# A decoder layer on one core: the gate projection as seven products of block sums instead of eight, its bias laid into the banks first

## What is computed

```python
    h = h + rms_norm(jnp.einsum('bsf,fd->bsd', ff, w_down[i]), mlp_post_g[i])
    gate = jax.nn.sigmoid(jnp.einsum('bsd,de->bse', h, w_ple_gate[i]) + b_ple_gate[i])
    ple = jnp.einsum('bsp,pd->bsd', p[i], w_ple[i]) * gate
    h = h + rms_norm(ple, ple_post_g[i])
```

## Time and profile before

| | |
|---|---|
| median of three runs | 583.5 us |
| the profiled execution: its span from first to last instruction | 581.5 us |
| what the runs' median has beyond that span | 2.0 us |
| TensorE / its weight loads busy | 573.5 / 500.8 us |
| VectorE / ScalarE / POOL busy | 495.2 / 356.4 / 98.6 us |
| first matmul of the gate, end of the last | 529.5, 575.4 us |
| from there to the end of the span | 6.1 us |

### The profile page before, as it was taken

The page is one execution under the profiler, slowest core; times in us unless marked ns, Lnnn a source line. Parts: engine busy times, 40 slices in busy tenths (PEclk is TensorE's granted clock), DMA queues, the critical chain, the costliest instruction groups (busy, mean ns, idle before and its releaser), DMA issues.

```text
span 581.5 us, 8919 instructions
## 1 busy us (share of the span) xinstructions
PE 573.5 (99%) x3400; PEld 500.8 (86%) x3400; DVE 495.2 (85%) x639; ACT 356.4 (61%) x569; POOL 98.6 (17%) x152
## 2 busy tenths in 40 slices
PE   8999999999999999999999999999999999999995
PEld 7888888888888888989999999999989999988885
DVE  5899986688766998999989999999999899799664
ACT  6896675775646746667656665575655756654422
POOL 0331536000103463001010011010100100011011
PEclk9999999999999999999999999999999999999998
DMA  8982008223003559469485492774753936584011
GB/s 269 345 320 85 0 2 324 76 72 123 25 1 109 202 189 319 87 183 229 96 249 114 119 276 41 215 185 74 264 132 75 285 75 155 207 294 178 0 73 73
DMA packets 26250, 89.26 MB, mean 154 GB/s; under 512 B 3040, under 2 KB 4448, under 8 KB 25696
## 3 DMA queue, kind: packets, MB, share of 16 engines
q1 hardware_dynamic: 20448, 66.59, 32.6%
q0 software_dynamic: 4032, 14.68, 14.3%
q10 hardware_dynamic: 1728, 7.42, 3.4%
HBM read 82.40 MB, written 6.29 MB: 153 GB/s over the span
## 4 chain that ended last, share of the span: by engine, by line
PE 98%; DMA 1%; DVE 0%; ACT 0%; SPq 0%; issue 0%; POOL 0%; DVEq 0%; ACTq 0%
PE psum L2340 31%; PE psum L2344 30%; PE psum L2345 30%; PE psum L2395 2%; PE psum L2578 2%; PE psum L2558 2%; DMA first_raw_a<-weights_dram 1%; PE psum L2409 1%; PE psum L2432 0%; DVE h L1323 0%; ACT w_hi L1393 0%; POOL stat L2192 0%; PE psum L2463 0%; PE psum L2457 0%; PE psum L2437 0%
## 5 line engine op out<-in xcount | busy, mean ns | idle before, releaser
L2340 PE MATMUL psum<-t_hi,a_hi 128*128 128x512 f32 x216 | 84.8, 393 | 0.0
L2344 PE MATMUL psum<-t_lo,a_hi 128*128 128x512 f32 x216 | 84.6, 392 | 0.0
L2345 PE MATMUL psum<-t_hi,a_lo 128*128 128x512 f32 x216 | 84.0, 389 | 0.0
L2340 PE MATMUL psum<-w_hi,actT_hi 128*128 128x512 f32 (+1 forms) x190 | 73.6, 387 | 0.0
L2345 PE MATMUL psum<-w_hi,actT_lo 128*128 128x512 f32 (+1 forms) x190 | 72.4, 381 | 0.0
L2344 PE MATMUL psum<-w_lo,actT_hi 128*128 128x512 f32 (+1 forms) x190 | 72.3, 380 | 0.0
L2345 PE MATMUL psum<-sum_hi,up_lo 128*128 128x256 f32 x224 | 63.4, 283 | 0.0
L2344 PE MATMUL psum<-sum_lo,up_hi 128*128 128x256 f32 x224 | 63.4, 283 | 0.0
L2340 PE MATMUL psum<-sum_hi,up_hi 128*128 128x256 f32 x224 | 63.2, 282 | 0.0
L2345 PE MATMUL psum<-actT_hi,up_lo 128*128 128x256 f32 (+1 forms) x200 | 60.0, 300 | 0.0
L2344 PE MATMUL psum<-actT_lo,up_hi 128*128 128x256 f32 (+1 forms) x200 | 60.0, 300 | 0.0
(11 more groups left out here) (264 smaller groups left out, 1415.8 us busy)
## 6 DMA issues: line engine op xcount, KB each, us to landing
raw<-weights_dram SPq DMA_DIRECT2D x34, 512.0 KB, 4.5
raw_o<-weights_dram SPq DMA_DIRECT2D x23, 512.0 KB, 4.3
raw_x<-weights_dram POOLq DMA_DIRECT2D x21, 512.0 KB, 5.6
raw_second<-weights_dram SPq DMA_DIRECT2D x14, 512.0 KB, 4.2
raw_x<-weights_dram SPq DMA_DIRECT2D x9, 512.0 KB, 5.9
qk_raw<-weights_dram SPq DMA_DIRECT2D x8, 512.0 KB, 6.8
gate_raw<-weights_dram SPq DMA_DIRECT2D x8, 512.0 KB, 5.1
raw_o<-weights_dram POOLq DMA_DIRECT2D x7, 512.0 KB, 7.1
```

What stands on the lines that cost most here:

```text
L2340: begin = nc.tensor.matmul(out, a_hi, b_hi, start=first, stop=False, skip_group_check=read_between)
L2344: nc.tensor.matmul(out, a_hi, b_lo, start=False, stop=False, skip_group_check=read_between)
L2345: return nc.tensor.matmul(out, a_lo, b_hi, start=False, stop=last, skip_group_check=read_between)
```

## The change

**The scheme.** h (turned) is cut in 2 x 2 blocks of 256 tokens x 512 k, A11, A12, A21, A22, and the weights in 2 x 2 blocks of 512 x 512. Seven products of blocks and block sums take the place of eight: GATE_11, 21, T1, T2, T3, T4, 22, the T ones with sums of weights. A product is worked for one pair member j of a token half at a time (128 tokens x 512 columns, 12 matmuls), and these 14 halves alternate by `GATE_PRODUCTS`. The last one, (6, 1), is cut in two parts of 256 columns.

**Sums of h.** ScalarE copies each turned bank to SBUF (`h2_copy_raw`) and splits six of the eight (`h2_split_hi`); VectorE's low parts now come from SBUF (`h2_split_lo`). VectorE makes E, S2, S3 and S4 for both j (`h2_sum`), ScalarE and VectorE split each (`h2_sum_split_hi`, `h2_sum_split_lo`).

**Sums of weights.** They are made by loads that add into what is there: four blocks (T1, T2, T3, T4) of two halves, issued by POOL (`add_gate`), each behind VectorE's split of the block before it (T3 behind a plain load), and standing among the four `down_rstd`. Splits are 128x1024 (`gate_split_hi`, `gate_split_lo`), 14 of them.

**Results.** The bias is copied by ScalarE into four banks ahead of the products (`seed_chain`, `seed_e`; POOL adds the two halves of the bias row once), and `gate_bias` is gone. Instead ScalarE drains six banks to `acc` (`gate_copy`), VectorE adds or subtracts (`gate_c11`, `gate_c22`), and `gate_fold` subtracts from banks in place. The nine sigmoid tiles keep their sizes and now come in another order, and token tiles end in the order 2, 0, 3, 1 (`TOKENS_DONE`). `gate_ple`, `gain_ple`, `square_ple`, the roots and `add_ple` are as before for each tile.

**Loads.** The gain row of the MLP, the bias row and the gain row of the embedding have places of their own and are loaded by SP; both ple loads and the last gain row are asked for once the down tiles are complete.

```diff
-GATE_TILES = ((0, 0, W), (1, 0, W), (0, W, W), (1, W, W), (2, 0, W), (2, W, W), (3, 0, W),
-              (3, W, W // 2), (3, W + W // 2, W // 2))
+GATE_TILES = ((0, 0, W), (1, 0, W), (2, W, W), (2, 0, W), (3, W, W), (0, W, W), (3, 0, W),
+              (1, W, W // 2), (1, W + W // 2, W // 2))
+TOKENS_DONE = (2, 0, 3, 1)
...
+GATE_PRODUCTS = ((0, 0), (1, 0), (0, 1), (1, 1), (2, 0), (3, 0), (2, 1), (4, 0), (3, 1), (5, 0), (4, 1), (6, 0),
+                 (5, 1), (6, 1))
...
             # VectorE
+            def h2_sum(which, j):
+                a11, a12, a21, a22 = h2_block(0, 0, j), h2_block(0, 1, j), h2_block(1, 0, j), h2_block(1, 1, j)
+                if which == OF_E:
+                    dve.wait_ge(h2_raw, 6 + 2 * j)
+                    first, second, how = a21, a22, ALU.subtract
...
+                nc.vector.tensor_tensor(gate_sum_source(which, j), first, second, how).then_inc(x_summed, 1)
+            def gate_c11(j):
+                dve.wait_ge(c_copied, gate_copy_at(COPY_C11, j))
+                dve.wait_ge(up_filled, gate_at(1, j))
+                part = acc[:, j, 0:W]
+                nc.vector.tensor_tensor(part, part, psum[:, GATE_P1 + j, :], ALU.add).then_inc(c_summed, 1)
...
-            for i, (t, c0, width) in enumerate(GATE_TILES):
-                gate_bias(i)
...
+            gate_c11(0)
+            gate_split_lo(GATE_T3, 0)
+            gate_split_lo(GATE_T3, 1)
...
+            h2_sum(OF_S3, 1)
+            gate_split_lo(GATE_T4, 0)
...
+            gate_ple(3)
+            gate_c22(1)
+            add_ple(2)
+            gate_ple(4)
+            gain_ple(4)
+            gate_ple(5)
+            add_ple(0)
+            gate_ple(6)
+            add_ple(3)
+            gate_ple(7)
+            gain_ple(7)
+            gate_ple(8)
+            add_ple(1)
...
             # ScalarE
+            def h2_copy_raw(i):
+                t, k_half = divmod(i, 2)
...
+                nc.scalar.activation(h2_block(t // 2, k_half, t % 2), h2_turned(i), ACT.Copy).then_inc(h2_raw, 1)
...
+            gate_copy(COPY_E, 0)
+            gate_copy(COPY_CHAIN, 0)
+            gate_split_hi(GATE_T4, 0)
...
+            for i in range(4, len(GATE_TILES)):
                 sigmoid(i)
                 square_ple(i)
...
             # POOL
+            add_gate(GATE_T1, 0)
+            add_gate(GATE_T1, 1)
+            pool.wait_ge(bias_loaded, 16)
+            nc.gpsimd.tensor_tensor(gate_bias_row[:, W:2 * W], gate_bias_row[:, 0:W], gate_bias_row[:, W:2 * W],
+                                    ALU.add).then_inc(bias_summed, 1)
+            add_gate(GATE_T2, 0)
+            down_rstd(0)
+            add_gate(GATE_T2, 1)
+            down_rstd(1)
+            down_rstd(2)
+            add_gate(GATE_T3, 0)
+            down_rstd(3)
+            add_gate(GATE_T3, 1)
+            add_gate(GATE_T4, 0)
+            add_gate(GATE_T4, 1)
...
             # TensorE
+            turn_h2(6)
+            turn_h2(7)
+            for i, j in GATE_PRODUCTS[4:-1]:
+                gate_product(i, j)
+            gate_product(6, 1, 0)
+            gate_product(6, 1, 1)
```

More of the change, by code:

```diff
@@ L1338, in _ @@
             tail_down(1)
-            splits(SLAB_GATE + 6)
+            gate_split_lo(GATE_T1, 1)
             tail_down(2)
@@ L1342, in _ @@
             tail_down(3)
-            splits(SLAB_GATE + KD)
+            gate_split_lo(GATE_21, 0)
             tail_down(4)
@@ L1367, in _ @@
-            for i, (t, c0, width) in enumerate(GATE_TILES):
-                gate_bias(i)
-                if i == SEEDED - 6:
-                    dve.wait_ge(*drained["gate", i])
-                    seed_bias()
-                gate_ple(i)
-                if i == gate_tiles_of(t)[-1]:
-                    add_ple(t, *gate_tiles_of(t))
-                else:
-                    gain_ple(i)
+            gate_split_lo(GATE_T2, 0)
+            gate_split_lo(GATE_T2, 1)
+            h2_sum(OF_E, 0)
@@ new lines, in _ @@
+            gate_split_lo(GATE_T4, 1)
+            gate_c11(1)
+            h2_sum(OF_S4, 0)
+            gate_fold(0)
+            gate_c22(0)
+            h2_sum_split_lo(OF_S3, 1)
+            h2_split_lo(7)
+            h2_sum(OF_S4, 1)
+            h2_sum_split_lo(OF_S4, 0)
+            gate_split_lo(GATE_22, 0)
+            gate_split_lo(GATE_22, 1)
+            gate_ple(0)
+            gain_ple(0)
+            h2_sum_split_lo(OF_S4, 1)
+            gate_fold(1)
+            gate_ple(1)
+            gain_ple(1)
@@ new lines, in _ @@
+            h2_sum_split_hi(OF_S3, 0)
+            h2_sum_split_hi(OF_S2, 1)
+            gate_copy(COPY_E, 0)
+            gate_copy(COPY_CHAIN, 0)
+            gate_split_hi(GATE_T4, 0)
+            gate_split_hi(GATE_T4, 1)
+            h2_sum_split_hi(OF_S3, 1)
+            gate_copy(COPY_E, 1)
+            sigmoid(0)
+            h2_sum_split_hi(OF_S4, 0)
+            gate_split_hi(GATE_22, 0)
+            gate_split_hi(GATE_22, 1)
+            h2_sum_split_hi(OF_S4, 1)
+            gate_copy(COPY_CHAIN, 1)
```

475 lines of the change are left out of this document (334 added, 141 removed).

## The result

The changed kernel takes 594.18 us (median of four runs, 593.15 to 595.08) against 583.64 us before, measured beside it: a ratio of 1.018, with a 95% interval of 1.016 to 1.020. It is slower, as forecast, but by 10.5 us and not by 3.9, and 594.2 lies above the range. The profiled execution took 593.49 us, its span is 591.7.

What follows compares the result with a forecast made beforehand. It took TensorE to bound the kernel before, and VectorE's queue to gate_ple(3) at 564.1 plus a 21.3 us chain afterwards: span 585.4, +3.9 over 581.5, plus 2.0 to the runs' median gives 587.4 us; range 585.4 to 590.4.

Steps and rivals of the forecast that it cites:

- the mechanism: Gate to end: TensorE loses 5.6 us of matmuls, but VectorE's queue and serial token tiles make the span 3.9 us longer; 77%.
- That queue: VectorE's instructions from 535.7 on, laid end to end (12.9, 9.4 and 5.3 us plus a 0.8 wait), reaching gate_ple(3) at 564.1.
- The chain behind it: From gate_ple(3) to the end: three token tiles one behind another instead of beside matmuls, 21.3 us.
- The 14 us of span behind the last matmul: Expected sign at the end: TensorE's last matmul at about 571, with 14 us of span after it instead of 6.
- One step inside the 6.2: Tile 8's multiply to the end: 5.65 us as before, with the last square starting 0.55 later because its root is late.
- the two terms without a row: Folds reading and writing a bank at once cost 0.60 and 0.37 us; VectorE's bank reads cost no more than SBUF reads.
- T3's second accumulating load: On POOL's queue behind down_rstd(3): issued at 533.3, landed at 540.7, costing VectorE 0.2 us at most.
- rival 2: The predicted chain plus T3's accumulating load late: 590.2 at 3 us late, 594.8 at 7.6 late; chance 15%.
- Rival 1: TensorE stays the bound through the gate and the time falls, to 578 to 579.5 us; chance 5%.

Runs made afterwards that it cites:

- e8: e6 with block 22's plain loads ahead of the ple loads and one POOL addition for the last root made earlier; 585.39 us, ratio 1.004.
- e12: e8 with ScalarE's first half of T4's split ahead of two result copies; 584.68 us, ratio 1.002.
- e6: e5 with the tail reordered: next tile's multiply and gain ahead of add_ple, each sigmoid ahead of the square before it; 585.7 us, ratio 1.005.
- e5: Changed kernel with the bias summed on VectorE and ple and gain loads held until T3's accumulating loads landed; 588.44 us, ratio 1.008.
- e2: Changed kernel with SP's ple and gain loads (2.5 MB) held until both accumulating loads of T3 landed; 588.73 us, ratio 1.009.
- e9: Changed kernel with only block 22's plain loads moved ahead of the ple and gain loads; 588.3 us, ratio 1.008.
- e1: Changed kernel with the two bias rows summed by VectorE instead of POOL; 593.75 us, ratio 1.016.
- e13: Changed kernel with only ple_late_b's load held until T3's accumulating loads landed; 589.06 us, ratio 1.009.
- e4: Kernel before the change with four unused 128x128 POOL multiplies added beside VectorE's splits; 583.5 us, ratio 1.000.
- e10: Changed kernel with POOL issuing T4's accumulating loads only after T3's have landed; 595.0 us, ratio 1.019.
- e11: Changed kernel with T3's second accumulating load issued ahead of down_rstd(3) on POOL's queue; 593.43 us, ratio 1.016.

## Why the prediction was right in sign and wrong in size

**Right: the mechanism.** TensorE gave up 5.6 us of matmuls and the time rose, since VectorE's longer queue and then three serial token tiles set the end. That queue, laid out end to end, was to bring `gate_ple(3)` at 564.1; with the two missed costs away it starts at 564.28 (e8) and 564.14 (e12), and at 564.09 in e6's profiled execution; in e5's, where T4's load is late, at 565.86. To the hundredth this is luck: VectorE is still 0.4 to 0.6 us late at `add_mlp(3)` in e6 and e8 (534.99, 535.18), and waits 0.46 at T4 where 0.8 was forecast. The chain behind it was to take 21.3 us and takes 21.25. Its parts in the changed kernel, from the starts of the multiplies: 4.04, 1.96, 3.91, 3.90, 1.26 and 6.2, against 3.9, 2.05, 3.9, 3.9, 1.35 and 6.2. The 14 us of span behind the last matmul were there too. One step inside the 6.2 does not add up: with tile 7's square ending at 578.5, as written, the last square would start 0.25 us later than it could, and not 0.55. The changed kernel shows 0.47 (it starts at 586.45, where the multiply of 585.52 allows 585.98).

**Right: the two terms without a row.** A bank read and written at once starts the next after 0.60 us in e5 (`gate_fold(0)` at 554.67, the next at 555.27), so the folds cost nothing extra. The Trainium skill (Perfetto Trace Analysis, "Optimizing Scalar/DVE Operations") has a higher overhead on banks; the new readers bear that out as little as the old rows did: an instruction on SBUF of the same shape also starts its next after 0.60 us (555.87 to 556.47 in e5).

**Wrong: T3's second accumulating load.** The prediction has it issued at 533.3 and landing 7.4 us later. The issue came at 535.4 and the landing 10.8 us after it, at 546.2. VectorE then stands for 3.52 us where the prediction had at most 0.2, and C22 waits 1.13 us more; with the ple and gain loads out of the way (e2, e9) 5 us and more come off. Its 7.4 was a sum for one load with a surcharge; what had to be asked is how many bytes are in flight beside it. The changed kernel puts 2.5 MB (ple_late_a, the gain, ple_late_b) on the engines 4 to 5 us before it, and the DMA share of the windows is 0.93 and 1.05. The row for it was there: ple_late_b took 7.8 us before, with 1 MB of gate_rows landing beside it in 7.9. By proportion, 2 MB in 7.8 us make 13.7 for the 3.5 MB of ple, gain and T3's loads (an estimate from that row): 543.9 counted from the first of them at 530.2. It is no lower bound, since part of the 7.8 is not transfer, and it leaves out what accumulating costs, which the queues show; but it says that 540.7 was not safe. The prediction used the 7.8 for the ple loads and never added up the bytes. What came is rival 2, held at 15%: the load 5.5 us later than the 540.7 assumed, between its points of 3 us (590.2) and 7.6 us (594.8). It was under-weighted by the same step.

**Wrong: POOL's addition, at nothing.** It stands in the change's code between two `add_gate` calls, and no term named it. It costs VectorE 1.83 us (1.23 to 3.06), of which 0.94 reach `add_mlp(3)` (e1, its offset taken off). Of the rest of the 1.96, 0.47 is the offset of the whole execution, and 0.46 the wait for POOL's root of token tile 3, which e1 keeps; the prediction had both queues alike up to there. Taken away alone the addition gives back 0.4 us in the medians, less than the runs scatter; e1's trace shows it swallowed by the load behind it.

**Not foreseen: TensorE's own loss.** The late load leaves TensorE idle for 3.5 us, since the sum it needs stands behind T3's splits on VectorE, and then at half its rate, and C22 waits 1.13 us for it. The prediction let rival 2 cost at most what the load was late.

**Rival 1 fell**, as held: no version came out under the kernel before. By the Trainium skill's rule (same page, "Identifying the Most-Contended Engine") the engine with the highest occupancy comes first, but for TensorE the page does not take the busy share of matmuls as the measure; it asks for the FLOP utilisation and the busy share of the weight loads. In the earlier trace rows the latter is 86% against VectorE's 85%, next to no lead; the prediction quotes the rule without this, and read by the 99% it points wrong here: TensorE's busy time fell by 1.9 us and the kernel lost ten.

**What is left of the loss.** Against the kernel before, median against median of the same comparison: 10.5 us for the changed kernel, 5.1 with the ple loads held back (e2), 5.3 with the bias moved as well (e5), 2.6 and 2.3 with the tail's order too (e6, e8), 1.1 at best (e12). With block 22's loads ahead of the ple loads alone it is 5.2 (e9), with one ple load held back 5.4 (e13). The bias's own share, with the load away, is thus not settled: e5's trace spends on T4's load what it gains on the bias. The last 1.1 us are likely the longer VectorE queue and POOL's roots, on which e12's VectorE still waits 1.34 us at the end; they were not taken apart, and no run shows it.

## What to carry to other kernels

Before a transfer that someone waits for is priced, count the bytes that are in flight beside it, those asked for just behind it from another queue too, and the share of the DMA engines in that window: here its landing went by those, and neither by its own issue nor by its median elsewhere. Loads that are not urgent go behind it, and one then looks at which load the held ones meet next. When the busiest engine is relieved, lay out the queue of the next one to the end of the program, since a chain that ran beside the matmuls can become the end of the span; and price every instruction on POOL by what VectorE's neighbours take beside it.

## What the runs showed of the hardware

- **POOL beside VectorE.** A POOL addition of 512 columns with both operands in SBUF lengthens a VectorE split of 128x1024 from 1.23 to 3.06 us (the changed kernel against e1). Beside four 128x128 multiplies two splits of 128x512 take 0.95 instead of 0.68, and one of 128x1024 keeps its 1.23 (e4). A copy from a bank beside POOL's additions keeps its 0.68 us (the kernel before, 212.05).
- **A 512 KB accumulating load** lands after 5.1 to 6.8 us with no ple load beside it (T3's in e2, e5, e6, e8, e9 and e12, T4's in e8, e9 and e12). T3's second half lands after 8.3 with 1.5 MB of plain loads ahead of it (e13), after 10.7 to 12.7 with 2.5 MB ahead, and then within 0.6 us of the last of these. T4's second half lands after 11.1 and 11.95 with 2.5 MB asked for up to 1.5 us behind it (e2, e5; block 22's 1 MB follows 4.7 us behind), and after 9.7 in e6's execution.
- **Two queues at once.** POOL's accumulating loads move 0.10 MB a microsecond beside SP's plain loads and 0.20 nearly alone (the changed kernel, 540 to 544 and 546 to 550).
- **TensorE's clock after a pause.** The windows table of the changed kernel and that of e13:

```profile
548.90:552.30 3.40, 0.00 (x0) 0.00 (x0) 3.37 (x6) 2.17 (x5) 0.00 (x0) 1.00 0.97 271
...
553.20:556.80 3.60, 3.60 (x11) 2.77 (x10) 3.14 (x4) 2.78 (x4) 0.00 (x0) 0.53 0.02 9
556.80:560.00 3.20, 3.20 (x15) 2.62 (x14) 2.07 (x5) 2.98 (x5) 0.00 (x0) 1.00 0.00 0
```

```profile
550.00:560.00 10.00, 10.00 (x46) 8.25 (x45) 9.54 (x14) 9.25 (x13) 0.00 (x0) 1.00 0.19 77
```

The granted clock is 0.53 from 553.2 to 556.8, the lower of its two levels (1.2 GHz), after TensorE did nothing from 548.9 to 552.4, and it is back at 2.4 GHz from 556.8 on. In e13 TensorE pauses for 1.0 us ahead of 549.2, and its clock stays at 1.00; in e10 and e11, with pauses of 3.4 us, and in e1, with one of 4.8, it falls as well. At 0.43 us a matmul instead of 0.23, the 3.6 us cost some 1.7.
